# A fourth 64-slot expert, and two of its 42 weight units multiplied as plain float32

## What is computed

```
def moe_swiglu(x, router, w_in, w_out):
    B, T, D = x.shape
    xt = x.reshape(B * T, D)
    logits = (xt @ router).astype(jnp.float32)
    top_v, top_i = lax.top_k(logits, MOE_TOP_K)
    top_w = jax.nn.softmax(top_v, axis=-1)
    gates = jnp.sum(jax.nn.one_hot(top_i, N_EXPERTS, dtype=jnp.float32) * top_w[..., None], axis=1)
    out = jnp.zeros_like(xt)
    for e in range(N_EXPERTS):
        out = out + gates[:, e:e + 1].astype(x.dtype) * swiglu(xt, w_in[e], w_out[e])
    return out.reshape(B, T, D)
```

## Time and profile before

| | us |
|---|---|
| median of 3 runs | 1469.05 |
| lowest, highest | 1467.59, 1470.61 |
| the profiled execution | 1468.5 |
| its span | 1466.7 |
| mean granted clock of TensorE | 0.993 |

### The profile page before, as it was taken

The page is one execution under the profiler, slowest core; times in us unless marked ns, Lnnn a source line. Parts: engine busy times, 40 slices in busy tenths (PEclk is TensorE's granted clock), DMA queues, the critical chain, the costliest instruction groups (busy, mean ns, idle before and its releaser), DMA issues.

```text
span 1466.7 us, 18711 instructions
## 1 busy us (share of the span) xinstructions
PE 1423.2 (97%) x7478; PEld 1207.5 (82%) x7478; DVE 1142.5 (78%) x795; ACT 961.6 (66%) x796; POOL 55.7 (4%) x66
## 2 busy tenths in 40 slices
PE   9999999999999999999999999999999999999996
PEld 9987789999889887887778887778887778888885
DVE  5456564545556598899998888999888999889886
ACT  5334544343444477778987777987777997777774
POOL 2001200000000021000002000001000000000000
PEclk9999999999999999999999999999999999999999
DMA  9654556555564469999999999999999999999990
GB/s 361 214 172 149 202 173 209 187 182 190 172 202 147 136 249 364 359 355 370 417 420 420 377 358 346 404 420 420 382 357 351 395 420 420 398 358 379 378 343 30
DMA packets 158743, 446.89 MB, mean 305 GB/s; under 512 B 7088, under 2 KB 46000, under 8 KB 158656
## 3 DMA queue, kind: packets, MB, share of 16 engines
q1 hardware_dynamic: 156832, 439.38, 80.5%
q0 software_dynamic: 1824, 6.33, 1.2%
HBM read 444.63 MB, written 1.05 MB: 304 GB/s over the span
## 4 chain that ended last, share of the span: by engine, by line
PE 73%; DVE 22%; ACT 2%; issue 2%; POOL 0%; DVEq 0%; ACTq 0%; POOLq 0%
PE ps L1422 21%; PE ps L1424 21%; PE ps L1423 21%; DVE wlo L964 13%; DVE wlo_more L964 4%; PE ps L1842 1%; PE ps L1843 1%; PE ps L1836 1%; PE ps L1759 1%; ACT whi L834 1%; PE ps L1879 1%; DVE h L1323 1%; DVE wlo L387 1%; PE ps L1468 1%; DVE y_lo L964 1%
## 5 line engine op out<-in xcount | busy, mean ns | idle before, releaser
L964 DVE TENSOR_TENSOR wlo<-raw,whi 128x2048 fp32r<-128x2048 f32 (+1 forms) x214 | 480.0, 2257 | 53.6 <-ACT whi L834 52.9
L834 ACT ACTIVATE whi<-raw 128x2048 fp32r<-128x2048 f32 x208 | 397.3, 1917 | 104.2 <-PE ps L1424 95.8
L387 DVE TENSOR_TENSOR wlo<-raw,whi 128x2048 fp32r<-128x2048 f32 x80 | 184.1, 2302 | 154.8 <-ACT whi L380 154.8
L380 ACT ACTIVATE whi<-raw 128x2048 fp32r<-128x2048 f32 x82 | 156.8, 1912 | 152.4 <-PE ps L1424 151.3
L1422 PE MATMUL ps<-whi,xg_big 128*128 128x512 f32 x420 | 166.1, 395 | 0.5 <-DVE wlo L964 0.5
L1424 PE MATMUL ps<-whi,xg_big 128*128 128x512 f32 x420 | 163.9, 390 | 0.0
L1423 PE MATMUL ps<-wlo,xg_big 128*128 128x512 f32 x420 | 163.7, 390 | 0.0
L1422 PE MATMUL ps<-xT_hi,whi 128*128 128x256 f32 x576 | 163.3, 284 | 0.0
L1424 PE MATMUL ps<-xT_hi,wlo 128*128 128x256 f32 x576 | 163.0, 283 | 0.0
L1423 PE MATMUL ps<-xT_lo,whi 128*128 128x256 f32 x576 | 163.0, 283 | 0.0
L1422 PEld LDWEIGHTS ps<-xT_hi,whi 128*128 128x128 f32 x576 | 110.5, 192 | 0.5
(11 more groups left out here) (253 smaller groups left out, 2750.7 us busy)
## 6 DMA issues: line engine op xcount, KB each, us to landing
raw<-in_moe_w_in SPq DMA_DIRECT2D x166, 1024.0 KB, 6.9
raw<-in_moe_w_out SPq DMA_DIRECT2D x86, 1024.0 KB, 7.8
more_raw<-in_moe_w_in SPq DMA_DIRECT2D x58, 1024.0 KB, 7.0
more_raw<-in_moe_w_out SPq DMA_DIRECT2D x26, 1024.0 KB, 7.7
raw<-in_ret_w_in SPq DMA_DIRECT2D x23, 1024.0 KB, 6.8
raw<-in_ffn_w_in SPq DMA_DIRECT2D x22, 1024.0 KB, 4.9
raw<-in_ffn_w_out SPq DMA_DIRECT2D x11, 1024.0 KB, 4.8
raw<-in_ret_w_out SPq DMA_DIRECT2D x8, 1024.0 KB, 4.9
```

Of the source, the lines that this page charges most:

```text
L380: nc.scalar.activation(whi[:, u % SPLIT, :], src, ACT.Copy).then_inc(hi_done, 1)
L387: nc.vector.tensor_tensor(wlo[:, u % SPLIT, :], src, whi[:, u % SPLIT, :].bitcast(F32), ALU.subtract).then_inc(lo_done, 1)
L834: nc.scalar.activation(moe_split(n)[0], moe_raw(n), ACT.Copy).then_inc(hi_done, 1)
L964: return nc.vector.tensor_tensor(dst, src, hi.bitcast(F32), ALU.subtract)
```

## The change

The sorted position 4 becomes a 64-slot position too, so that there are four of each kind and they alternate: jobs 1, 3, 5 and 7 are 64-slot. The last job is now one of them, and job 6 gathers for a 64-slot job only.

In each 64-slot job, units 10 and 22 are not split. ScalarE and VectorE pass over them, and TensorE multiplies the landed float32 numbers by the stationary tile read as plain float32: one matmul for each block of 512 columns, four for a unit. The place of a split unit is now chosen by the number of split units before it. A slot that held an unsplit unit is free when TensorE has used the unit (`unit_used`), and TensorE waits for the landing itself.

```
-    POSITION = [0, 5, 1, 6, 2, 7, 3, 4]
-    SMALL = [position >= 5 for position in POSITION]
+    POSITION = [0, 4, 1, 5, 2, 6, 3, 7]
+    FIRST_SMALL = 4
+    SMALL = [position >= FIRST_SMALL for position in POSITION]
...
+    SMALL_NATIVE = (10, 22)
...
+        SPLITS = [n for n in range(MOE_UNITS) if not (SMALL[n // JOB_UNITS] and n % JOB_UNITS in SMALL_NATIVE)]
+        S_AGAIN = U_MOE + len(SPLITS)
+        def native(n):
+            return n not in SPLITS
+        def splits(n):
+            return len([i for i in SPLITS if i < n])
...
         def moe_split(n):
-            s = n % MSPLIT
+            s = splits(n) % MSPLIT
...
+            def slot_free(n):
+                if n < RAW:
+                    sp.wait_ge(lo_done, U_MOE + n - RAW + 1)
+                elif n < MRAW:
+                    sp.wait_ge(h_ready, T * 2 + 1)
+                elif native(n - MRAW):
+                    sp.wait_ge(unit_used, U_MOE + n - MRAW + 1)
+                else:
+                    sp.wait_ge(lo_done, U_MOE + splits(n - MRAW) + 1)
...
             def moe_hi(n):
-                if n < MOE_UNITS:
+                if n < MOE_UNITS and not native(n):
                     moe_landed(act, n)
-                    if n != SPLIT:
-                        act.wait_ge(unit_used, U_MOE + n - (MSPLIT if n > SPLIT else SPLIT) + 1)
+                    order = splits(n)
+                    if order > SPLIT:
+                        act.wait_ge(unit_used, U_MOE + SPLITS[order - MSPLIT] + 1)
+                    elif order < SPLIT:
+                        act.wait_ge(unit_used, U_MOE + order - SPLIT + 1)
                     nc.scalar.activation(moe_split(n)[0], moe_raw(n), ACT.Copy).then_inc(hi_done, 1)
...
             def moe_lo(n):
-                if n < MOE_UNITS:
+                if n < MOE_UNITS and not native(n):
                     hi, lo = moe_split(n)
-                    dve.wait_ge(hi_done, U_MOE + n + 1)
+                    dve.wait_ge(hi_done, U_MOE + splits(n) + 1)
                     lo_of(lo, moe_raw(n), hi).then_inc(lo_done, 1)
...
             def gather_pair(j, k):
-                w = P if j + 2 >= JOBS else P + HALF
+                c, w = (P, HALF) if j + 2 >= JOBS else (0, P + HALF)
...
             def both(dst, a, hi, lo, start, stop):
+                if lo is None:
+                    return pe.matmul(dst, a.bitcast(F32), hi, start=start, stop=stop, skip_group_check=True)
                 pe.matmul(dst, a, hi, start=start, stop=False, skip_group_check=True)
                 return pe.matmul(dst, a, lo, start=False, stop=stop, skip_group_check=True)
...
-                pe.wait_ge(lo_done, u + i + 1)
+                if native(n):
+                    moe_landed(pe, n)
+                else:
+                    pe.wait_ge(lo_done, U_MOE + splits(n) + 1)
```

More of the change, by code:

```diff
@@ L71, in build @@
     HALF = P // 2
-    POSITION = [0, 5, 1, 6, 2, 7, 3, 4]
-    SMALL = [position >= 5 for position in POSITION]
+    POSITION = [0, 4, 1, 5, 2, 6, 3, 7]
+    FIRST_SMALL = 4
+    SMALL = [position >= FIRST_SMALL for position in POSITION]
     BIGS, SMALLS = SMALL.count(False), SMALL.count(True)
-    CAPACITY = [P] * 5 + [HALF] * 3
     FIRST_KEY = 1 << 14
-    assert not SMALL[0] and not SMALL[-1]
+    assert not SMALL[0] and SMALL[-1]
     BIG_SILU = {3: (0, 0), 4: (0, 1), 11: (1, 0), 12: (1, 1), 23: (2, 0), 24: (2, 1), 33: (3, 0)}
@@ L494, in _, with moe_unit @@
                 load_unit(sp, U_ATT_OUT + i, 0, att_out[:, 2 * i:2 * i + 2, :], 2)
-            def moe_unit(u, i, e, slot, dst, free, small=False):
+            def moe_unit(i, e, slot, dst, small=False):
                 src, rows = moe_source(i, e, small)
-                sp.wait_ge(lo_done, free)
                 sp.dma_start(dst.rearrange("p (k n) -> p k n", k=rows), src).then_inc(landed[slot], 16)
+            def slot_free(n):
[7 more added lines that the diff above has]
+                    sp.wait_ge(lo_done, U_MOE + splits(n - MRAW) + 1)
             def expert(position):
@@ L512, in _ @@
                     n = j * JOB_UNITS + i
[L513 to L517, removed]
+                    slot_free(n)
+                    moe_unit(i, e, moe_slot(n), moe_raw(n), SMALL[j])
             sp.wait_ge(over_ready, 1)
@@ L525, in _ @@
                         n = p * JOB_UNITS + i
[L526 removed]
+                        sp.wait_ge(lo_done, S_AGAIN + max(n - RAW + 1, 0))
+                        moe_unit(i, e, i % RAW, raw[:, i % RAW, :])
             for t in range(T):
@@ L1769, in gather_pair @@
                 else:
[L1770 to L1773, removed]
+                    pe.wait_ge(small_copied, j // 2 * KD + k)
+                gather_step(k, ps[:, 7, :], sel[:, j // 2 % 2, :, c:c + w], w).then_inc(gathered, 1)
             def turn_sel(job, chosen):
@@ L1794, in pieces, with big_unit @@
                 return [(4 * q + c, 0, c * BANK) for c in range(4)]
-            def big_unit(i, u, big, job, x, hi, lo, before_gate, before_up):
+            def big_unit(i, ready, big, job, x, hi, lo, before_gate, before_up):
                 part, b, q = BIG_STREAM[i]
@@ L1840, in both, with small_unit @@
             def both(dst, a, hi, lo, start, stop):
+                if lo is None:
+                    return pe.matmul(dst, a.bitcast(F32), hi, start=start, stop=stop, skip_group_check=True)
                 pe.matmul(dst, a, hi, start=start, stop=False, skip_group_check=True)
                 return pe.matmul(dst, a, lo, start=False, stop=stop, skip_group_check=True)
-            def small_unit(i, u, small, job, hi, lo, before_gate, before_up):
+            def small_unit(i, n, small, job, hi, lo, before_gate, before_up):
                 part, b, q = SMALL_STREAM[i]
@@ L1867, in small_unit @@
                             w = slice((2 * c + half) * BANK, (2 * c + half + 1) * BANK)
-                            last = both(ps[:, 4 + half, :], gT_small[b % 2][:, 2 * q + c, :], hi[:, w], lo[:, w],
+                            last = both(ps[:, 4 + half, :], gT_small[b % 2][:, 2 * q + c, :], hi[:, w], lo if lo is None else lo[:, w],
                                         b == 0 and q == 0 and c == 0, b == 3 and q == 1 and c == 1)
@@ L1921, in _ @@
                 for i in range(JOB_UNITS):
+                    n = j * JOB_UNITS + i
                     if j == 0 and i < 4:
@@ L1926, in _ @@
                     if SMALL[j]:
-                        small_unit(i, u, smalls, j, *moe_split(j * JOB_UNITS + i), before_gate, before_up)
+                        small_unit(i, n, smalls, j, *((moe_raw(n), None) if native(n) else moe_split(n)), before_gate,
+                                   before_up)
                         small_turn(i, smalls)
                     else:
-                        big_unit(i, u, bigs, j, xg_big[bigs % 2], *moe_split(j * JOB_UNITS + i), before_gate,
+                        big_unit(i, U_MOE + splits(n) + 1, bigs, j, xg_big[bigs % 2], *moe_split(n), before_gate,
                                  before_up)
```

32 lines of the change are left out of this document (16 added, 16 removed).

## The result

Six runs after the change have a median of 1461.2 us (1459.0 to 1462.4), six of the kernel before beside them 1469.8 (1467.6 to 1473.0). The ratio is 0.9942, 95% interval 0.9929 to 0.9954: **8.6 us faster**, where 17.7 were forecast, and 0.2 us above the top of the range. The profiled execution took 1461.47 us, its span 1459.7, 7.0 under the span before.

The account below looks back on a forecast made before the run. A 64-slot job was taken as bounded by TensorE, VectorE and the weight stream within 3 us. Job 7's 18.1 us saving less 0.4 for unsplit units gave 17.7 off, forecast 1451.3 us, range 1446 to 1461.

Parts of the forecast that it names:

- Job 7: Last expert job, made 64-slot: 119.7 to 101.6 us, 18.1 us off, bounds 16.4 to 19.3.
- What follows is unchanged: Stretch after TensorE's last matmul of job 7: stays at 15.0 us.
- TensorE's price of an unsplit unit: 64-slot jobs: four plain float32 matmuls of two instructions each, 3.44 us instead of 1.81, 1.63 more per unit.
- The late starts would absorb it, -0.8 per job: TensorE in 64-slot jobs: 3.3 us extra work against 4.1 us of late starts, net -0.8 per job.
- three late, three saved: End of a 64-slot job: landings 3 us later, VectorE's queue 2.7 us shorter, ScalarE's 0.3 us wait gone; net +0.1 per job.
- The next 128-slot job takes over no delay: Job behind a 64-slot one: uses a unit every 2.96 us against 2.51 per transfer, so no delay carried over.
- the one I put at 0.04: Rival, slower: SyncE's wait on units 10 and 22 delays all requests behind; in full +10.7 per job, 1493.8 us; chance 0.04.
- the unsplit units cost: Rival, 64-slot jobs: late starts not refilled as ScalarE's copies wait for TensorE, +1.5 to +3.3 per job, 1457 to 1464; 0.18.
- The relief pays: Rival, 64-slot jobs: hole after unit 10 closes, TensorE's path decides, -0.8 per job, 1447.7 us; chance 0.15.
- the lower stream rate: Rival, weight transfers: HBM binds at about 358 GB/s, a 64-slot job takes 123 us, total 1472; chance 0.01.
- Unit 22 leaves no hole: Request for unit 22's slot goes at 1165.3, not 1160.94; 11 us of queued transfers cover it, cost 0.
- Its signs in the profile: Expected: jobs 1, 3, 5 within 1 us, 32 x 2 float32 instructions, longer SyncE pause, ScalarE landing waits of several us.

Follow-up runs that it names:

- all units split: Changed kernel with the fourth 64-slot expert kept but no unsplit unit (SMALL_NATIVE empty): 1451.4 us, ratio 0.9869 to the kernel before.
- the wait alone: Changed kernel with every unit split, but SyncE's request for load 18 of each 64-slot job also waits until TensorE has used unit 11: 1462.7 us, ratio 0.9945.
- load 18 moved: Changed kernel, units 10 and 22 unsplit, with only the load into unit 10's slot issued two loads later in SyncE's order: 1452.8 us, ratio 0.9894.
- TensorE's work alone: Changed kernel with every unit split, plus 14 idle matmul instructions (1.5 us) after units 10 and 22 of each 64-slot job: 1454.6 us, ratio 0.9891.

## Why the prediction was right or wrong

**What bounds the kernel: right, and it decided.** A 64-slot job has three bounds within 3 us, and 3.8 us of relief for VectorE paid nothing while the stream was late.

**Job 7: the mechanism was right, the size 1.2 to 1.8 off.** Forecast 101.6 after 119.7; 102.9 with all units split, 103.4 after. Both are inside the bounds of 100.4 to 103.3 or 0.1 beyond. The 102.9 came at clock 0.97, the slowest of the three levels that the rows of before already showed, and the 103.4 at 0.98 holds the loss of the unsplit units as well.

**"What follows is unchanged": wrong by 1.0, and the cause is open.** Before, TensorE waited 2.09 us for the last y_lo, and its last scatters ran 0.23 apart. After, it waits 2.49, and they run 0.44 apart:

```profile
1453.91 0.49 PE L1785 MATMUL ps<-y_hi,selT 128*128 128x512 f32 x1 [2.09 <-DVE y_lo L964]
```
```profile
1446.23 0.65 PE L1806 MATMUL ps<-y_hi,selT 128*128 128x512 f32 x1 [2.49 <-DVE y_lo L987]
1446.67 0.63 PE L1807 MATMUL ps<-y_lo,selT 128*128 128x512 f32 x1
```

With all units split what follows takes 16.0 too, but there the scatters run 0.23 apart and start late, and the profile names nothing that TensorE waited for:

```profile
1437.34 0.49 PE L1806 MATMUL ps<-y_hi,selT 128*128 128x512 f32 x1 [3.10 <-issue]
```

In the kernels with a fourth 64-slot expert and no idle matmuls in the tail this stretch takes 15.4 to 16.9 us, one execution of each, against 15.0. The fourth expert alone took 19.1 us off the median (1470.5 to 1451.4, by the interval 15.7 to 22.8) and 16.6 off the profiled span; the 18.1 of the sum lies between.

**TensorE's price of an unsplit unit: right.** All 32 plain float32 matmuls are two instructions, and unit 10 takes from 1140.38 to about 1143.8, 3.44 us. The group of them, per instruction 592 ns with its way out:

```profile
L1864 PE MATMUL ps<-raw,xg_small x64: 590/592/593, 682.3 to 1399.4; 128*128 128x512 f32 x64
```

**The late starts would absorb it, -0.8 per job: right where the stream is in time.** Only unit 22 unsplit gives -0.7 to -0.9, units 22 and 34 -1.1.

**The step that failed: "three late, three saved", +0.1 per job.** Its parts, in the order of the sum, for job 5. The request for unit 10's slot (load 18) went out 6.6 us later, forecast 6.3. It landed 4.7 us after that, not 5.9 as before, which gave back 1.2, forecast 0.5. From there to load 24 the stream won back another 1.2, where the sum had 2.8. So load 24 landed 53.9 into the job, not 49.7, and load 42, the next job's first, at 99.0, not 94.7: 4.2 and 4.35 late, where I took "3 us later", and nothing was won back behind load 24. The rows are the requests with their time to landing: load 24 before and after, and load 42 before; load 42 after is the unit that ScalarE takes at 1210.30 above.

```profile
L499 SPq DMA_DIRECT2D raw<-in_moe_w_in x1: 376/376/376, 1147.1 to 1147.1; - x1
DMA to landing us min/median/max: 7.9/7.9/7.9
```
```profile
L510 SPq DMA_DIRECT2D raw<-in_moe_w_in x1: 377/377/377, 1154.0 to 1154.0; - x1
DMA to landing us min/median/max: 11.1/11.1/11.1
```
```profile
L499 SPq DMA_DIRECT2D raw<-in_moe_w_in x1: 373/373/373, 1188.6 to 1188.6; - x1
DMA to landing us min/median/max: 11.5/11.5/11.5
```

I had taken the whole unused 15% as there to be used. From load 18 to load 24 the landings came 2.92 us apart before and 2.72 after, not the 2.51 of the later stretch; why not, no run here shows.

The saving had the forecast size and the wrong cause. From load 42's landing to the end of its split it is 4.3 us, not 7.2, so 2.9 less. I had put that down to the two skipped splits. But with the wait alone, where no split is skipped, it is 4.3 us as well (landed at 99.07, split at 103.33 into its job 5, rows above): when the loads come late, VectorE's queue is gone by itself. So the relief saved nothing; the first 2.9 us of lateness were hidden by that queue, and the rest came out at the job's end. 4.35 less 2.9 is 1.4, which is job 5's +1.4 at equal clock.

Jobs 1, 3 and 5 of the profile show 6.3. At equal clock, by the levels of the kernel with every unit split, they lose 1.45, 1.8 and 1.4; job 1 also went from clock 1.00 to 0.97 (worth 2.8), and job 3 from 0.97 to 0.98 (worth -1.2). Four jobs make about 6 instead of 0.4.

**"The next 128-slot job takes over no delay": wrong, +0.9 each.** I compared rates (2.96 us a unit against 2.51), and a rate says nothing of the first units: they are late, the result of the job before is drained behind them, and the scatter with it; the chain of after goes from the late landing over these steps to the scatter. The 0.9 is there with the wait alone (125.52) and gone wherever load 18 isn't held up (124.5 to 124.8).

**The sum of the two:** about 6 and 0.9 x 3, so 8 to 9 us by the lengths, 9.8 by the medians (1461.2 against 1451.4), that the forecast had at 0.4. That is the 9.1 by which the gain fell short, to within the noise; what the fourth expert gave lies around its 18.1.

**The rivals.** The one that came true in mechanism is the one I put at 0.04: SyncE's wait on TensorE's use of a unit holds up every request behind it. I priced it only with both delays in full, 10.7 per job, and put its threshold at 4.5. Its real price is 2.1 to 2.3 per 64-slot job, with the 128-slot job behind it, by their lengths (8.4 to 9.1 in all), 2.8 by the medians (1462.7 with the wait alone, 1451.4 without, in four), under the threshold; between "nothing" and "in full" I had no case. The one with the right time but a wrong reason is "the unsplit units cost" (1457 to 1464): it had late starts not refilled because ScalarE waits for TensorE, and unit 22, where that would act too, gains. "The relief pays" is true, but only for units whose slots the stream doesn't miss. For the lower stream rate: the later stretch again moved 417 GB/s over 58.9 us, so the Trainium skill's statement (DMA: Bandwidth & Descriptors, "Where 436 GB/s comes from") that the HBM side binds at about 358 for transfers from HBM didn't hold here. The same section gets the 358 by dividing the bandwidth of a stack by two cores; this kernel runs on one core.

**Unit 22 leaves no hole: right.** Its slot's load is asked for with some 11 us of transfers queued; only-22 keeps 398 GB/s at clock 1.00. There was little room to spare: in its job 5 load 30 goes out 4.6 us later than in the kernel before (60.2 into the job, not 55.5) and lands 5.1 us after that, so the queue had just run down.

**Its signs in the profile.** The 32 x 2 instructions and the longer pause in SyncE's requests came, and ScalarE now waits for nearly every landing at the job's end. Jobs 1, 3 and 5 did not stay within 1 us, and job 1 passed the mark of 2 us (4.3), 2.8 of it by the clock.

**What stays open.** Why the stream won back 1.2 us and not 2.8; what lengthens the stretch behind job 7; why the clock stays at 1.00 in some waits of 2.9 us and falls in others; and whether the kernel before gains from the idle matmuls too, which wasn't tried.

## What to carry to other kernels

When a buffer's release moves from an early consumer to a later one, follow the request that reuses it through its in-order queue: if the stream behind has no work in hand at that point, most of the delay reaches every later landing (here 4.2 to 4.35 of 6.6 us), and little of a queue's unused share before the pause can be counted against it (1.2 us of 2.8). Work taken from an engine whose input comes late saved nothing here. Put such a step where transfers are queued (here unit 22 or 34 instead of 10: some 13 us), or send that one request later, but only so far that it still lands ahead of its use. Price each rival at the middle as well as in full.

## What the hardware showed that I had not expected

After the same wait of 2.9 us at its start, a 64-slot job with every unit split takes 100.45, 102.03 or 103.27 us, with a granted clock of 1.00, 0.98 or 0.97: three levels, nothing between, in another order in each of the two executions profiled. With idle matmuls in the wait it was 1.00 in all twelve profiled jobs, and with units 22 and 34 unsplit that is worth 1.6 us a job, against 1.1 for the two unsplit units together. It can be 1.00 without them too: all four jobs had it in the kernel with load 18 moved. Placed where TensorE only reaches them after the wait, they ran at the low clock and cost their full 4 us.

A good part of the difference between executions comes from further up. Just ahead of job 0, the kernel before and the one with unsplit units alone:

```profile
513.60:529.10 15.50, 14.98 (x132) 14.56 (x130) 13.37 (x32) 8.09 (x11) 0.00 (x0) 1.00 0.23 81
```
```profile
515.40:535.50 20.10, 19.57 (x131) 19.19 (x130) 14.85 (x33) 9.23 (x11) 0.00 (x0) 0.76 0.30 108
```

The same 130 matmuls took 15.5 us at 1.00 and 20.1 at 0.76, in code that no kernel here changed. The profiled executions of only unit 10 and of TensorE's work alone have the same low stretch (0.76), and they are the slowest of their kernels, by 4.0 and 5.6 us. What brings it about isn't shown. Whoever compares two medians of this kernel has to look at this stretch first: it is worth more than several of the terms above.
